# Value product of the 16-key tail of the prompt heads: one matmul over stacked parts in place of three

## The reference

```python
s = jnp.einsum('nqhd,nkhd->nhqk', q, k, preferred_element_type=jnp.float32) * (HEAD_DIM ** -0.5)
s = s + (c_q... - c_k...)                      # forgetting: cumulative log gates
s = jnp.where(causal[None, None], s, NEG_INF)
p = jax.nn.softmax(s, axis=-1)
return jnp.einsum('nhqk,nkhd->nqhd', p.astype(v.dtype), v)
```

## Time and profile before

| | |
|---|---|
| median of 3 runs | 2520.35 us (2518.38 to 2520.36) |
| profiled execution, span from the first to the last instruction | 2517.1 us, and the page gives no time outside of it |
| TensorE matmuls busy | 2496.6 us (99%), 18268 instructions |
| TensorE weight loads busy | 2462.9 us (98%) |
| VectorE busy | 1818.8 us (72%) |
| ScalarE busy | 1049.5 us (42%) |
| granted TensorE clock | 1.000 of full speed |

### The profile page before, as it was taken

One profiled execution on the slowest core, in us unless ns is written; L12 is line 12 of the kernel. 1 busy time (PEld: TensorE's weight loads), 2 busy tenths in 40 slices (PEclk: granted clock), 3 DMA queues, 4 the chain that ended last, 5 costly groups with the idle time before them and its releaser, 6 DMA issues. The chain is left out here.

```text
span 2517.1 us, 45832 instructions
## 1 busy us (share of the span) xinstructions
PE 2496.6 (99%) x18268; PEld 2462.9 (98%) x18268; DVE 1818.8 (72%) x2467; ACT 1049.5 (42%) x1494; POOL 24.1 (1%) x48
## 2 busy tenths in 40 slices
PE   8999999999999999999999999999999999999999
PEld 8999999999999999999999999988999999999999
DVE  6434437766678998964445798988786666899987
ACT  4111124333343333355335787776653333333333
POOL 0000000000000000000000100010000000000000
PEclk9999999999999999999999999999999999999999
DMA  4111110333353313015424566645323333443112
GB/s 131 42 42 50 42 43 26 128 103 104 104 181 133 104 69 103 18 52 170 129 81 128 148 145 167 153 127 183 96 80 103 103 103 104 178 138 126 64 52 70
DMA packets 249037, 259.41 MB, mean 103 GB/s; under 512 B 18144, under 2 KB 184192, under 8 KB 248898
## 3 DMA queue, kind: packets, MB, share of 16 engines
q1 hardware_dynamic: 229510, 248.26, 31.8%
q10 hardware_dynamic: 19388, 9.20, 1.3%
HBM read 193.86 MB, written 63.42 MB: 102 GB/s over the span
## 5 line engine op out<-in xcount | busy, mean ns | idle before, releaser
L872 PE MATMUL ps<-h_op,w_op 128*128 128x268 f32 x4912 | 614.2, 286 | 0.2
L872 PEld LDWEIGHTS ps<-h_op,w_op 128*128 128x128 f32 x4912 | 609.6, 188 | 0.6 <-DVE w_op L912 0.6
L605 PE MATMUL ps<-x_hi,w_hi 128*128 128x358 f32 x1248 | 279.9, 330 | 2.0 <-DVE w_lo L589 1.7
L605 PE MATMUL ps<-x_hi,w_lo 128*128 128x358 f32 x1248 | 275.5, 327 | 0.0
L605 PE MATMUL ps<-x_lo,w_hi 128*128 128x358 f32 x1248 | 275.0, 326 | 0.0
L589 DVE TENSOR_TENSOR w_lo<-w_raw,w_hi 128x1024 fp32r<-128x1024 f32 x76 | 92.8, 1222 | 250.8 <-ACT w_hi L581 250.8
L883 ACT ACTIVATE w_op<-w_op_f 128x2048 fp32r<-128x2048 f32 (+1 forms) x54 | 97.6, 1808 | 381.6 <-PE ps L872 361.5
L605 PEld LDWEIGHTS ps<-x_hi,w_hi 128*128 128x128 f32 x1248 | 213.3, 189 | 5.0 <-DVE w_lo L589 2.2
L605 PEld LDWEIGHTS ps<-x_lo,w_hi 128*128 128x128 f32 x1248 | 215.8, 189 | 0.0
L605 PEld LDWEIGHTS ps<-x_hi,w_lo 128*128 128x128 f32 x1248 | 215.6, 189 | 0.0
L1069 DVE TENSOR_TENSOR t<-ps,t 128x536 f32<-128x536 f32 x180 | 128.7, 715 | 119.3 <-PE ps L817 110.4
(11 more groups left out here) (377 smaller groups left out, 5165.6 us busy)
## 6 DMA issues: line engine op xcount, KB each, us to landing
raw_a<-in_mlp_w SPq DMA_DIRECT2D x120, 256.0 KB, 3.1
h_op_f<-h_rows SPq DMA_DIRECT2D x24, 1072.0 KB, 6.6
w_op_f<-in_mlp_w SPq DMA_DIRECT2D x24, 1024.0 KB, 7.5
h_rows<-t SPq DMA_DIRECT2D x90, 268.0 KB, 2.1
w_raw<-in_conv_w_in SPq DMA_DIRECT2D x24, 512.0 KB, 3.8
w_raw<-in_w_kv SPq DMA_DIRECT2D x16, 512.0 KB, 4.8
w_raw<-in_w_o SPq DMA_DIRECT2D x16, 512.0 KB, 3.8
k_page<-in_cache_k SPq DMA_DIRECT2D x16, 512.0 KB, 4.6
```

Source lines behind the costliest of these rows:

```text
L605: mm = pe.matmul(PS[:, bank(s, g), 0:GW], w[:, s, k], x[:, k, g * GW:(g + 1) * GW], start=(at == 0 and n == 0), stop=(at == KC - 1 and n = ...
L872: mm = pe.matmul(PS[:, 2 * p + g, 0:QW], w[:, k, P * m:P * m + P], x[:, k, QW * g:QW * g + QW], start=(k == 0 and j == 0), stop=(k == tile ...
```

## The change

For the tail, the three products become one over stacked parts. The contraction runs over 80 rows (STACK): rows 0 to 15 (TAIL_HI) hold the high part of the 16 values against the high part of the probabilities, rows 32 to 47 (TAIL_HI2) the low part of the values against the high part of the probabilities, and rows 64 to 79 (TAIL_LO) the high part of the values against the low part of the probabilities. The rows between are zero. So the 16 raw value rows are loaded three times, into three places of the last tile of VRAW (or OT), with one semaphore for the four DMAs (64 in place of 32 per load). values_hi rounds the whole tile as before. values_lo makes the low parts of the eight full tiles in one instruction and that of rows 32 to 47 in place in VH in another. ScalarE writes the rounded exponential three times in place of once, and the float32 one to rows 64 to 79. VectorE subtracts in rows 64 to 79. tail_ones clears one probability tile in place of two and writes the ones to two places per head parity in place of one.

```diff
@@ -187,6 +187,8 @@
 CHUNK_OF = [x[0][0] for x in GROUPS]
 CHUNK_END = [max(g for g in range(NG) if CHUNK_OF[g] == c) for c in range(len(CHUNKS))]
 TAIL = min(P, NPR - P * (NT - 1))
+TAIL_HI, TAIL_HI2, TAIL_LO = (slice(x, x + TAIL) for x in (0, 32, 64))
+STACK = 64 + TAIL
 
 
 USES = ["M", (1, 0, 144), (2, 0, 272), (3, 0, 400), (4, 16, 528), (5, 0, 512), (5, 512, 656), (6, 0, 512), (6, 512, 784),
@@ -405,8 +407,7 @@
         PBH = put("probs_hi", [P, HI_RING, 768], F32R)
         PBL = put("probs_lo", [P, HI_RING, 768], F32R)
         PF8 = put("tail_f32", [P, 2, TAIL])
-        P8H = put("tail_hi", [P, 2, TAIL], F32R)
-        P8L = put("tail_lo", [P, 2, TAIL], F32R)
+        P8S = put("tail_hi_hi_lo", [P, 2, TAIL], F32R)
         INV = put("inv_sums", [P, NPR])
         OS = put("o_and_sums", [P, 2, NPR])
         SM = put("sums_spread", [65, 2, 16])
@@ -1238,12 +1239,14 @@
             ge(act, l_done, ops_done(t - 2))
             act.activation(wide(PF[:, t % 2], t), wide_logits(t), ACT.Exp, scale=SCALE).then_inc(e_done, 1)
             if g == NG - 1:
-                act.activation(PF8[0:TAIL, h % 2], PS[0:TAIL, 2 * (t % 2) + 1, 0:TAIL], ACT.Exp, scale=SCALE)\
+                act.activation(PF8[TAIL_LO, h % 2], PS[0:TAIL, 2 * (t % 2) + 1, 0:TAIL], ACT.Exp, scale=SCALE)\
                    .then_inc(e_done, 1)
             ge(act, pv_done, t - 2)
             act.activation(wide(PBH[:, t % HI_RING], t), wide_logits(t), ACT.Exp, scale=SCALE).then_inc(h_done, 1)
             if g == NG - 1:
-                act.activation(P8H[0:TAIL, h % 2], PS[0:TAIL, 2 * (t % 2) + 1, 0:TAIL], ACT.Exp, scale=SCALE)\
+                for rows in (TAIL_HI, TAIL_HI2):
+                    act.activation(P8S[rows, h % 2], PS[0:TAIL, 2 * (t % 2) + 1, 0:TAIL], ACT.Exp, scale=SCALE)
+                act.activation(P8S[TAIL_LO, h % 2], PS[0:TAIL, 2 * (t % 2) + 1, 0:TAIL], ACT.Exp, scale=SCALE)\
                    .then_inc(h_done, 1)
 
         def probs_lo(t):
@@ -1256,7 +1259,7 @@
             dve.tensor_tensor(PBL[:, (t + 2) % HI_RING, 0:nb * w], PF[:, t % 2, 0:nb * w],
                               PBH[:, t % HI_RING, 0:nb * w].bitcast(F32), ALU.subtract).then_inc(l_done, 1)
             if g == NG - 1:
-                dve.tensor_tensor(P8L[0:TAIL, h % 2], PF8[0:TAIL, h % 2], P8H[0:TAIL, h % 2].bitcast(F32),
+                dve.tensor_tensor(P8S[TAIL_LO, h % 2], PF8[TAIL_LO, h % 2], P8S[TAIL_LO, h % 2].bitcast(F32),
                                   ALU.subtract).then_inc(l_done, 1)
 
         def v_raw(m):
@@ -1267,7 +1270,7 @@
 
             m, hh = head(h)
             own, _ = halves(hh)
-            act.wait_ge(v_loaded, 32 * (m + 1))
+            act.wait_ge(v_loaded, 64 * (m + 1))
             ge(act, pv_done, NG * (h - 1))
             act.activation(VH[:, hh, :, own], v_raw(m)[:, :, own], ACT.Copy).then_inc(v_hi, 1)
 
@@ -1276,8 +1279,10 @@
             m, hh = head(h)
             own, _ = halves(hh)
             dve.wait_ge(v_hi, h + 1)
-            dve.tensor_tensor(VL[:, hh, :, own], v_raw(m)[:, :, own], VH[:, hh, :, own].bitcast(F32), ALU.subtract)\
-               .then_inc(v_lo, 1)
+            dve.tensor_tensor(VL[:, hh, 0:NT - 1, own], v_raw(m)[:, 0:NT - 1, own], VH[:, hh, 0:NT - 1, own].bitcast(F32),
+                              ALU.subtract)
+            low = VH[TAIL_HI2, hh, NT - 1, own]
+            dve.tensor_tensor(low, v_raw(m)[TAIL_HI2, NT - 1, own], low.bitcast(F32), ALU.subtract).then_inc(v_lo, 1)
 
         def weigh_values(t, uses=()):
 
@@ -1290,13 +1295,15 @@
             pe.wait_ge(l_done, ops_done(t))
             for c, j, q0, n, keys, bank, col in GROUPS[g]:
                 a, x = q0 - CHUNKS[c][0], WIDE[g][1] * bank + col
-                ph, pl = (PBH[:, t % HI_RING, x:x + n], PBL[:, (t + 2) % HI_RING, x:x + n]) if keys == P else \
-                    (P8H[:, h % 2], P8L[:, h % 2])
                 to = PS[:, 6 + (3 * h + c) % 2, a:a + n]
                 last = g == CHUNK_END[c] and j == GROUPS[g][-1][1]
-                pe.matmul(to, VH[:, hh, j], ph, start=(j == 0), stop=False)
-                pe.matmul(to, VL[:, hh, j], ph, start=False, stop=False)
-                mm = pe.matmul(to, VH[:, hh, j], pl, start=False, stop=last)
+                if keys < P:
+                    mm = pe.matmul(to, VH[0:STACK, hh, j], P8S[0:STACK, h % 2], start=False, stop=last)
+                else:
+                    ph, pl = PBH[:, t % HI_RING, x:x + n], PBL[:, (t + 2) % HI_RING, x:x + n]
+                    pe.matmul(to, VH[:, hh, j], ph, start=(j == 0), stop=False)
+                    pe.matmul(to, VL[:, hh, j], ph, start=False, stop=False)
+                    mm = pe.matmul(to, VH[:, hh, j], pl, start=False, stop=last)
                 done = j == GROUPS[g][-1][1]
                 if done:
                     mm.then_inc(pv_done, 1)
@@ -1593,7 +1600,8 @@
                 f = slice(P * m, P * m + P)
                 sp.dma_start(v_raw(m)[:, 0:NT - 1], vp[0:full, f].rearrange("(t p) c -> p t c", p=P))\
                   .then_inc(v_loaded, 16)
-                sp.dma_start(v_raw(m)[0:LASTP, NT - 1], vp[full:NPR, f]).then_inc(v_loaded, 16)
+                for rows in (TAIL_HI, TAIL_HI2, TAIL_LO):
+                    sp.dma_start(v_raw(m)[rows, NT - 1], vp[full:NPR, f]).then_inc(v_loaded, 16)
 
             def load_head(h):
 
@@ -2025,12 +2033,12 @@
             for hh in range(2):
                 _, other = halves(hh)
                 dve.memset(VH[:, hh, NT - 1, other].bitcast(F32), 0.0).then_inc(v_zero, 1)
-            dve.memset(P8H[:, :, :].bitcast(F32), 0.0).then_inc(v_zero, 1)
-            dve.memset(P8L[:, :, :].bitcast(F32), 0.0).then_inc(v_zero, 1)
-            dve.wait_ge(v_zero, 6)
+            dve.memset(P8S[:, :, :].bitcast(F32), 0.0).then_inc(v_zero, 1)
+            dve.wait_ge(v_zero, 5)
             for hh in range(2):
                 _, other = halves(hh)
-                dve.memset(VH[0:LASTP, hh, NT - 1, other].bitcast(F32), 1.0).then_inc(v_zero, 1)
+                for rows in (TAIL_HI, TAIL_LO):
+                    dve.memset(VH[rows, hh, NT - 1, other].bitcast(F32), 1.0).then_inc(v_zero, 1)
 
         def mask_rows():
 
@@ -2114,7 +2122,7 @@
                 if t == 1:
                     pe.wait_ge(unit_read, U_O)
                 if t == 5:
-                    pe.wait_ge(v_zero, 8)
+                    pe.wait_ge(v_zero, 9)
                 logits(t + 2)
                 use_ahead(h, g)
                 weigh_values(t, uses_of(h, g))
```

## The result

The changed kernel takes 2527.94 us (median of 5 runs, 2527.27 to 2529.55) against 2519.41 for the kernel before in the same sitting: ratio 1.0036, 95% interval 1.0026 to 1.0047. The forecast was 2517.7, its range ended at 2521.2: it is slower by 8.5 us, where 2.6 less were expected.

What follows compares the result with a forecast made beforehand. TensorE, busy 99%, was taken to bound the attention over the prompt; -3.6 (pairs) + 0.4 (VectorE) + 0.1 (set-up memset) + 0.5 (value load) = -2.6 us, so 2517.7 us, range 2515.0 to 2521.2.

Steps and rivals of the forecast that it cites:

- TensorE's pairs, -3.6: Attention tail: two of three load-and-matmul pairs go, 0.226 us per head over 16 heads, -3.6 us.
- 0.06 us of the engine each, 0.13 per head: ScalarE's tail group: price of two more 16x16 activations per head, bounds 0.12 and 0.32 us.
- that idle time hides it: ScalarE's waits for row-maximum shifts, 2.4 us a head, cover the added activations; without that cover 2 us.
- Net +0.07 us per head (bounds 0.05 and 0.15): VectorE's split values_lo: big part saves 0.066 us, small one costs 0.14; hidden by idle time in most stretches.
- Heads 1 to 4, +0.4: VectorE's room in heads with leftover normalisation and staging is 0.5 to 0.95 us: loss +0.4 us, bounds 0 and 1.2.
- The value load, +0.5: SP queue: three tail DMAs land 0.3 us later, delaying ScalarE's value split; only the worst load loses, +0.5 us.
- TensorE is not what is waited for: Rival: VectorE and ScalarE set the heads' pace, pairs give nothing; 2520.3 to 2521.5, say 2520.5 us; chance 0.10.
- Emptying at 80 rows: Rival: TensorE empties where the row count changes, 0.29 us a head; +2.0, 2522.4 us; chance 0.04.

Runs made afterwards that it cites:

- e9: Kernel before with two more small ScalarE activations per head in the tail group, at rows 0 to 15, read by nothing: +0.55 us.
- e7: Kernel before with only VectorE's small subtraction of the tail's probabilities moved to rows 64 to 79: +3.2 us.
- e3: Kernel before with the tail's two small ScalarE activations reading PSUM rows 64 to 79, still writing rows 0 to 15: +3.0 us (2522.12).
- e2: Kernel before with the tail's probabilities moved to rows 64 to 79 on ScalarE (two activations) and VectorE (one subtraction): 2525.66 us against 2519.12, +6.5.
- e16: Changed kernel with VectorE's 128x416 tail-group subtraction no longer waiting for the small activations: 2523.74 us, +5.4 against the kernel before.
- e15: Changed kernel with all small probability and value instructions at rows 0 to 15 and one 16-row tail load: 2517.58 us, -1.4 against the kernel before.
- e12: e8 with a single tail load and GpSimd's low part of the next head's tail values ahead of its copies: 2516.14 us against 2518.38 before.
- e17: e12 with VectorE's 128x416 tail-group subtraction no longer waiting for the small activations: 2514.93 us against 2518.39 for the kernel before.
- e4: Changed kernel with another stack order, low part at rows 0, high part at rows 32 and 64: 2523.48 us, +4.4 against the kernel before.
- e5: Changed kernel with its small probability instructions all at rows 0 to 15, value part and loads unchanged: 2520.74 us, +2.1 against the kernel before.
- e10: Kernel before with the three tail loads and the split value subtraction, its small part at rows 32 to 47: +3.3 us.
- e13: Kernel before with the split value subtraction, its small part at rows 32 to 47, and one 80-row tail load: +2.6 us.
- e14: Kernel before with the value subtraction split, the small part at rows 0 to 15, load as before: +0.5 us.
- e11: Changed kernel with one 80-row tail load per value tile in place of three loads: 2527.54 us.
- e8: Changed kernel with ScalarE and VectorE at rows 0 to 15, GpSimd making the stack's copies and low value part: 2517.76 us, -0.9 against before.

## Why the prediction was wrong

Plain heads (the median distance from the sixth on, without the last, as in all heads' distances above), beside the stretch from the start of ScalarE's tail chain to the row-maximum shift, both read from the timelines:

| kernel | chain's end | VectorE run | stretch | heads apart |
|---|---|---|---|---|
| before | 1.04 | 3.43 | 4.69 | 15.83 |
| e9, count | 1.17 | 3.43 | 4.80 | 15.82 |
| e7, VectorE's place | 1.03 | 3.68 | 4.91 | 15.90 |
| e3, ScalarE's place | 1.46 | 3.43 | 5.09 | 16.11 |
| e2, both | 1.45 | 3.68 | 5.33 | 16.32 |
| e16 | 1.68 | 3.72 | 5.18 | 16.17 |
| after | 1.67 | 3.68 | 5.56 | 16.56 |
| e15, stacked, all at rows 0 | 1.16 | 3.43 | 4.79 | 15.80 |
| e12, stacked, GpSimd | 1.04 | 3.45 | 4.69 | 15.70 |
| e17, e12 and the wait moved | 1.04 | 3.44 | 4.61 | 15.61 |

(The chain's end counts from its start; the run goes from the start of the 128x416 subtraction to the end of the row maximum.) One rule fits these rows to 0.02: a head takes 15.83 - 0.14 us plus what the stretch is above 4.69, but no less than TensorE's own time, 15.83 with three pairs and 15.60 with one. For the changed kernel: 15.69 + 0.87 = 16.56. The 0.14 is read from these rows, and the 15.60 is worked out from the pairs (15.83 - 0.226); no kernel here is faster. e4 (stretch 5.17, heads 16.18) and e5 (4.79, 15.78) fit as well. e10 and e13 don't: with a stretch of 4.79 they should take 15.83 and take 15.92. e16 and e17 test it: they were run after the others, with their distances forecast as 16.12 and 15.62 from the same circle, and have 16.17 and 15.61.

*TensorE's pairs, -3.6: the engine's part right, its worth wrong.* One pair holds 0.11 us and nothing empties around 80 rows. But a second limit lay 0.14 us below TensorE's, so of 0.226 a head only 0.14 could come through; e12 has 0.13, e15 0.03 with its two activations more, and e17, with the second limit shortened by 0.08, has 0.22.

*ScalarE, the step that failed: "0.06 us of the engine each, 0.13 per head", "that idle time hides it".* The price of the count was right, and free (e9). The change also moved the tail's activations to rows 32 and 64, which I cost at nothing; with it the chain grew by 0.64 us (end at 1.67 instead of 1.04) and not by 0.13. And its cover was not the 2.4 us a head in which ScalarE waits for shifts. In the tail group ScalarE's end releases VectorE, VectorE's run ends in the row maximum, and TensorE's shift of that releases ScalarE again. In the kernel before ScalarE waits there, behind the group:

```profile
1558.81 0.37 ACT L1186 ACTIVATE q_hi_ext<-ps 1x256 fp32r<-1x256 f32 x1 [1.24 <-PE ps L1118]
```

These 1.24 us are a wait for what the group itself sets going (the shift at 1558.31), so they move with it and cover nothing. The room in this circle was 0.14 us.

*VectorE, "Net +0.07 us per head (bounds 0.05 and 0.15)".* The split costs nothing at rows 0 (e14) and 2.6 us at rows 32 (e13). The moved tail subtraction was left out of the working; it lengthens VectorE's run from 3.43 to 3.68 us and costs 3.2 us alone (e7). Both borders belong in this term.

*Heads 1 to 4, +0.4.* They grew by 0.51, 0.35, 0.36 and -0.04 us, 1.2 in all, although TensorE has 0.226 less to do in each. As the prediction counts it, as a loss from that gain, this is 1.2 + 0.9 = 2.1 us, five times the +0.4 and above its upper bound of 1.2.

*The value load, +0.5.* The fear was of late parts; e11 shows that three loads or one of 80 rows are the same. ScalarE waits for value loads 1.6 us in three pieces, where 2.3 us stood before the worst one alone in my forecast, and the late head of before (17.00) is gone in the changed kernel (16.57). What makes a head late is not shown: with heads as short as before, e9, e13 and e14 have none above 16.0 among the plain ones, while e12 has one of 16.77 and e4, with three loads, two of 17.48 and 17.41.

*The rivals.* "TensorE is not what is waited for" (0.10) was the mechanism, but I priced it by the count of the added work. Emptying at 80 rows did not happen.

The trace of before shows the rule that I missed. VectorE's division writes rows 0 to 63 for even heads and 64 to 127 for odd ones; odd, then even:

```profile
1527.51 0.15 DVE L1160 TENSOR_REDUCE row_max<-ps 16x1 fp32r<-16x16 f32 x1
1527.70 1.24 DVE L1331 TENSOR_TENSOR q_all<-o_and_sums,inv_sums 64x1040 f32<-64x1040 f32 x1
1528.97 0.31 DVE L1170 CUSTOM_DVE_ANT_0 masked_short<-ps,mask_wide_next 128x144 f32<-128x144 f32 x1
...
1543.33 0.15 DVE L1160 TENSOR_REDUCE row_max<-ps 16x1 fp32r<-16x16 f32 x1
1543.41 1.22 DVE L1331 TENSOR_TENSOR q_all<-o_and_sums,inv_sums 64x1040 f32<-64x1040 f32 x1
1544.56 0.29 DVE L1170 CUSTOM_DVE_ANT_0 masked_short<-ps,mask_wide_next 128x144 f32<-128x144 f32 x1
```

For the odd head it starts 0.19 us behind the 0.15 us reduction and the next one 1.27 behind its 1.24; for the even head 0.08 behind, and the next one 1.15 behind its 1.22. The same instruction costs 0.23 us more by its place (0.11 ahead of it and 0.12 behind). The Trainium skill, page VectorE: DVE Perf Modes, section Two Vector instructions with no wait between them, says that a VectorE instruction starts only when all earlier ones have finished if its input begins in another group of 32 partitions than the last one read from that memory, or its output in another than the last one written to it. These rows, e7 and e13 agree with it: 0.20 to 0.23 us for an instruction that goes there and back. Worked in for the two moved instructions, it would have made VectorE's term about 0.5 us a head and not 0.07; with my belief in over 1 us of idle time that would still have been hidden in most heads. ScalarE's part of the loss doesn't follow from it.

What stays open: how e13's 0.1 us a head reaches TensorE (its stretch of 4.79 us would leave the head at TensorE's 15.83, so it is another place of the head), and why the first tail load comes 1.6 us later in the changed kernel (1428.98 against 1427.39), of which 1.3 come back behind the last head; in e2 to e10 and e12 to e17 it comes between 1427.84 and 1429.24. A difference of e5, e8, e9, e14 or e15 to before is inside its interval, and those of e12 and e13 reach its edge; for these the distances in the trace carry the reading.

## What to carry to other kernels

Cost a moved small instruction by its place too: on ScalarE and VectorE, put small instructions in the same group of rows as their neighbours, and let an idle engine make the copies that a stack needs. Idle time of an engine is no cover where it is a wait for something that the added work delays; read the room in that circle of waits (when the result is ready against when it is taken up), not the engine's sum. And a busy share of 99% says nothing of how near the second limit is: here it was 0.14 us a head away, less than the gain.

## What I had not expected of the hardware

ScalarE loses the overlap by a change of place as VectorE does, and a change of the input's place in PSUM alone is enough (e3): a 16x16 activation holds the engine 0.065 us between neighbours at its own rows, and 0.27 more when it reads or writes rows 64 to 79 between neighbours at rows 0. Three DMAs of 8 KB and one of 40 KB that reads the same 16 rows five times make no difference that can be measured here (2527.94 and 2527.54; +3.3 in e10 and +2.6 in e13); neither was run against a single one of 8 KB with all else equal. GpSimd's two copies and one subtraction a head, beside ScalarE and VectorE, cost neither of them anything that shows: chain 0.94 us and run 3.45 in e12.
